# Differential attention two heads at a time, its scores in three banks

## The chip, the core and the metric

The kernel runs on one core of a Trainium2 chip. Its engines have queues of their own and meet at semaphores: TensorE (PE in the profile, its weight loads PEld), VectorE (DVE), ScalarE (ACT), GpSimd (POOL) and SyncE (SP), which issues the loads. The metric is the device time of one launch in microseconds.

## The reference

Two layers of two kinds of attention side by side, and after them a block with a convolution, pooling, cross attention and a feed-forward part, for 256 tokens of width 2048. The change touches the differential attention of the two layers alone: eight heads, each with two maps of 64 wide queries and keys, whose softmaxes are subtracted.

```python
def one_block(start):
    qb = lax.dynamic_slice_in_dim(q, start, BLOCK_Q, axis=1)
    s = jnp.einsum('bqhmd,bkhmd->bmhqk', qb, k).astype(jnp.float32) * scale
    ...
    s = jnp.where((dist >= 0)[None, None, None], s + bias[None, None], NEG_INF)
    p = jax.nn.softmax(s, axis=-1)
    w = p[:, 0] - lam * p[:, 1]
    return jnp.einsum('bhqk,bkhd->bqhd', w.astype(v.dtype), v)
```

The second attention (`_mla_attention`, called MLA below) takes its queries and keys from two latents of rank 512, `c_q` and `c_kv`, each times a weight matrix.

## The kernel before, in words

All weights stream through TensorE in units of 128 x 1024. SyncE loads a unit, ScalarE rounds it (`w_hi`, L406), VectorE subtracts (`w_lo`, L411), and TensorE multiplies in three passes (L448 to L450, L491 to L493). Four slots are reused in turn, and ScalarE and VectorE work three units ahead of TensorE. Products gather in `acc`, four banks in two pairs. A chunk of products takes the pair its number gives (even or odd), and may start only when an engine has evacuated the chunk two before it and counted it in `acc_free0` or `acc_free1` (`banks_free`).

A layer has 56 units for queries, keys, values and gate, then a loop of 32 steps, then 32 steps for the gate of MLA (z 0 to 31 here), then 32 for the output. The attention runs in the cracks of this stream. In the loop of 32 steps (u below, one unit each) TensorE multiplies: u 0 to 15 the latents, u 16 and 17 the rope key, u 18 to 21 the queries of MLA (one chunk each: 9, 10, 11, 12), u 22 and 23 the rope part of the queries, u 24 to 27 its keys (chunks 14 to 17), u 28 and 29, and u 30 and 31, its values (chunks 18, 19). ScalarE evacuates the query and key chunks with `copy_cols`, one step after the product. So u 20 (chunk 11) waits for the copy of u 18's chunk 9, and u 28 (chunk 18) for the copy of u 26's chunk 16.

Behind each unit stands what attention needs, written out by hand for each engine in the same loop. In the kernel before, head h takes four steps, u = 4h to 4h + 3:

- u = 4h: TensorE turns the last head's three weight blocks (L1152) and this head's two key blocks (L541); ScalarE copies both to SBUF.
- u = 4h + 1: TensorE multiplies the last head's weights with its values (L1158 to L1160) and makes this head's scores, two maps of 64 rows each in two banks (L1175). VectorE scales them, adds the bias and takes the maxima (`diff_max`, L2127 to L2135).
- u = 4h + 2: ScalarE takes the exponentials (L1694), where it stands in its queue behind the rounding of that step.
- u = 4h + 3: VectorE mixes the two maps (`diff_weights`, L2141 to L2147).

Everything that TensorE does between two units is called a burst below. Of the four banks of `aux`, `tb` (bank 0) holds turned blocks, `sc1` and `sc0` (banks 1, 2) the scores and `pv` (bank 3) turned weights and outputs. The latents are turned at u 10, 11, 19 and 21 (`C_TURN`), the rope key is summed on VectorE at u 17, just ahead of `diff_max`, and turned in `pv` at u 21.

The evacuation that the prediction speaks of, and its place in ScalarE's loop:

```python
for u in range(32):
    if u - 1 in QUERY_COLS:
        copy_cols(u - 1, C_QUERY + QUERY_COLS[u - 1], query_pair(QUERY_COLS[u - 1]))
    if u - 1 in KEY_COLS:
        copy_cols(u - 1, C_KEY + KEY_COLS[u - 1], key_pair(KEY_COLS[u - 1]))
    ...
    rounded(U_QKV + u)
    ...
    if r == 2:
        exps(h, ...)
```

Of the kernel before, what the change touches and what calls it, by code (L numbers as in the profile page):

```python
# [26 lines left out]
AX_X = mybir.AxisListType.X  # L27
# [76 lines left out]
TB_LAYER = 30  # L104
# [3 lines left out]
DIFF_TB = [2, 3, 4, 7, 8, 10, 12, 13]  # L108
C_TURN = {10: (0, 0, 5), 11: (0, 1, 6), 19: (1, 0, 9), 21: (1, 1, 11)}
QR_TB = 14  # L110
KEY_HEAD = 4
GATE_TURN = {12: (0, 0, 16), 13: (0, 1, 17), 20: (1, 0, 18), 21: (1, 1, 19), 28: (2, 0, 20), 29: (2, 1, 21),
             36: (3, 0, 22), 37: (3, 1, 23)}
X_TB = 24
MLA_PAIRS = HEADS // 2
# [3 lines left out]
HEAD_LAYER, PV_LAYER = HEADS + MLA_PAIRS, 2 * HEADS + 2 * MLA_PAIRS  # L119
# [132 lines left out]
def build(nc, dram, out):  # L252
# [12 lines left out]
    with ctx:  # L265
# [23 lines left out]
        kT = turn_f32[:, 1, 0:SEQ]  # L289
# [51 lines left out]
        roped, pool_step = sem("roped"), sem("pool_step")  # L341
        scores_ready, row_max, exps_done = sem("scores_ready"), sem("row_max"), sem("exps_done")
# [294 lines left out]
        s = b1("s", [P, 3 * SEQ])  # L637
        pT = b1("pT", [P, 2, 3 * P])
        lam_l = b1("lam_l", [P, 1])
        neg_max = b1("neg_max", [P, 4])  # L640
        row_sum = b1("row_sum", [P, 4])
        inv_sum = b1("inv_sum", [P, 4])
        mix_f = b1("mix_f", [P, 2])
# [221 lines left out]
        with nc.Block() as block:  # L865
# [136 lines left out]
            def _(pool):  # L1002
# [25 lines left out]
                for layer in range(LAYERS):  # L1028
# [5 lines left out]
                    pool.wait_ge(pv_free, layer * PV_LAYER + (2 * KEY_HEAD + 2))  # L1034
                    pool.wait_ge(tb_filled, layer * TB_LAYER + (TB_PRO + DIFF_TB[5] + 1))
# [27 lines left out]
                pool.wait_ge(row_max, (LAYERS - 1) * HEAD_LAYER + HEADS)  # L1063
# [19 lines left out]
            def _(pe):  # L1083
# [55 lines left out]
                for layer in range(LAYERS):  # L1139
# [7 lines left out]
                    def turn_weights(n, cols):  # L1147

                        if n > 0:
                            pe.wait_ge(pv_free, pv0 + n)  # L1150
                        for i, col in enumerate(cols):
                            mm = pe.transpose(pv[:, i * P:(i + 1) * P], s[:, col:col + P], ident[:, :])  # L1152
                        mm.then_inc(pv_filled, 1)
# [8 lines left out]
                    def outputs(n, val):  # L1162

                        pe.wait_ge(pv_free, pv0 + n)
                        weighted(0, 0, val).then_inc(pv_filled, 1)

                    def diff_scores(h):

                        pe.wait_ge(tb_free, tb0 + (DIFF_TB[h] + 1))
                        if h > 0:  # L1170
                            pe.wait_ge(row_max, head0 + h)
                        for col, q, keys in ((0, 1, SEQ), (SEQ, 0, P)):
                            for m, bank in ((0, sc1), (1, sc0)):
                                e = slice(m * DQ, (m + 1) * DQ)
                                mm = pe.matmul(bank[:, col:col + keys], diff_query(h)[e, q * P:(q + 1) * P],  # L1175
                                               kT[e, 0:keys], start=True, stop=True)
                        mm.then_inc(scores_ready, 1)

                    def diff_turn_weights(h):
                        pe.wait_ge(probs_ready, layer * HEADS + (h + 1))  # L1180
                        turn_weights(2 * h, (0, P, 2 * SEQ))

                    def diff_outputs(h):
                        outputs(2 * h + 1, lambda k: kz[:, k, WIDTH + h * DV:WIDTH + (h + 1) * DV])

                    def mla_scores(p):

                        if p == 0:
                            evacuated(pe, pairs, C_KEY + 2)
                            evacuated(pe, pairs, C_KEY + 3)  # L1190
                            pe.wait_ge(tb_free, tb0 + QR_TB + 2)
                            pe.wait_ge(pv_free, pv0 + 2 * HEADS)
                        pe.wait_ge(row_max, head0 + (HEADS + p))
# [20 lines left out]
                    def mla_turn_weights(p):  # L1214

                        pe.wait_ge(rsum_ready, layer * MLA_PAIRS + (p + 1))
                        pe.wait_ge(pv_free, pv0 + (2 * HEADS + 2 * p))
                        for i, bank in ((0, sc0), (1, pv)):
                            for n, col in enumerate((i * SEQ, i * SEQ + P, 2 * SEQ + i * P)):
                                mm = pe.transpose(bank[:, n * P:(n + 1) * P], s[:, col:col + P], ident[:, :])  # L1220
                        mm.then_inc(pv_filled, 1)

                    def mla_outputs(p):
# [4 lines left out]
                        pe.wait_ge(pv_free, pv0 + (2 * HEADS + 2 * p + 1))  # L1228
                        for i in range(2):
                            mm = weighted(i, i * SEQ, lambda k: value_of(2 * p + i, k))  # L1230
                        mm.then_inc(pv_filled, 1)

                    def diff_block(h):
                        return lambda i: kz[:, i, h * DV:(h + 1) * DV]
# [105 lines left out]
                    for u in range(32):  # L1340
# [22 lines left out]
                        h, r = u // 4, u % 4  # L1363
# [5 lines left out]
                        if r == 0:  # L1369
                            if h > 0:  # L1370
                                diff_turn_weights(h - 1)
                            turn(pe, tb0 + DIFF_TB[h], diff_block(h), blocks=2)
                        if r == 1:
                            if h == KEY_HEAD + 1:
                                pe.wait_ge(pv_free, pv0 + (2 * KEY_HEAD + 1))
                                evacuated(pe, pairs, 8)
                                for t in range(T):
                                    pe.matmul(pv[:, 3 * P + t * ROPE:3 * P + (t + 1) * ROPE],
                                              key_sum[:, t * P:(t + 1) * P], key_fold, start=True, stop=True)
                            if h > 0:  # L1380
                                diff_outputs(h - 1)
                            diff_scores(h)
                        if u in C_TURN:
                            j, t, use = C_TURN[u]
                            evacuated(pe, pairs, 6 + j)
# [4 lines left out]
                    for u in range(32):  # L1390
# [4 lines left out]
                        if u == 0:  # L1395
                            diff_turn_weights(HEADS - 1)
                            pe.wait_ge(roped, layer + 1)
                            turn(pe, tb0 + QR_TB, lambda i: qr[:, i % 2, (i // 2) * P:(i // 2 + 1) * P])
                        if u == 1:

                            pe.wait_ge(pv_free, pv0 + (2 * HEADS - 1))
                            for t in range(T):
                                pe.transpose(pv[:, (2 + t) * P:(3 + t) * P], kr2[:, t, :], ident[:, :])
                            diff_outputs(HEADS - 1)
# [3 lines left out]
                    for u in range(32):  # L1408
# [3 lines left out]
                        if u in (0, 6):  # L1412
                            pe.wait_ge(tb_free, tb0 + (22 if u == 0 else 23))
                        product_rows(pe, base, U_QKV + 64 + u, mT, 2 * i, 2, 512, c % 2, i == 0, i == 7,
                                     (lambda: pe.wait_ge(tb_free, tb0 + 24)) if u == 6 else None)
# [213 lines left out]
            def _(act):  # L1629
# [39 lines left out]
                for layer in range(LAYERS):  # L1669
# [28 lines left out]
                    def copy_weights(n):  # L1698

                        act.wait_ge(pv_filled, pv0 + (n + 1))  # L1700
                        if n < 2 * HEADS:
                            act.activation(pT[:, 0, :], pv[:, 0:3 * P], ACT.Copy).then_inc(pv_free, 1)
                        else:
                            act.activation(pT[:, :, :], aux[:, 2:4, 0:3 * P], ACT.Copy).then_inc(pv_free, 1)

                    def diff_output(h):


                        act.wait_ge(pv_filled, pv0 + (2 * h + 2))
                        for t, col, r in ((1, 0, 0), (0, P, 2)):  # L1710
                            o_step(act.activation(junk[:, 0:P], pv[:, col:col + P], ACT.Square,
                                                  scale=inv_sum[:, r:r + 1],
                                                  accum_out=sumsq_o[:, T * h + t:T * h + t + 1]))
                        for t, col, r in ((1, 0, 0), (0, P, 2)):
                            ins = act.activation(diff_output_of(h, t), pv[:, col:col + P], ACT.Copy,
                                                 scale=inv_sum[:, r:r + 1])
                        if h == KEY_HEAD:
                            for t in range(T):
                                ins = act.activation(kr[:, t, :], pv[:, 3 * P + t * ROPE:3 * P + (t + 1) * ROPE], ACT.Copy,
                                                     scale=rstd[:, t:t + 1])  # L1720
                        if h == HEADS - 1:
                            ins = act.activation(krT[:, :], pv[:, 2 * P:4 * P], ACT.Copy)
                        ins.then_inc(pv_free, 1)

                    def mla_output(p):

                        act.wait_ge(pv_filled, pv0 + (2 * HEADS + 2 * p + 2))
# [6 lines left out]
                    def z_heads(u):  # L1734

                        if u in MLA_TURN:
                            copy_weights(2 * HEADS + 2 * MLA_TURN[u])
                        if u in MLA_OUT:
                            mla_output(MLA_OUT[u])
                        if u - 1 in MLA_SCORE:  # L1740
                            exps(HEADS + MLA_SCORE[u - 1],
# [66 lines left out]
                    for u in range(32):  # L1808
# [17 lines left out]
                        h, r = u // 4, u % 4  # L1826
                        if r == 0:
                            if h > 0:
                                copy_weights(2 * (h - 1))
                            copy_bank(DIFF_TB[h], kT, tb[:, 0:SEQ])  # L1830
                        if r == 1 and h > 0:
                            diff_output(h - 1)
# [893 lines left out]
```

## Time and profile before

| | |
|---|---|
| median of 3 runs | 1917.46 us (1917.41 to 1917.61) |
| the profiled execution | 1917.76 us, its span 1915.6 us |
| granted TensorE clock over the span | 0.999 |
| TensorE matmul busy | 1906.9 us, 100% |
| VectorE, ScalarE, GpSimd busy | 75%, 56%, 3% |
| DMA | mean 189 GB/s |

Spans are read from starts: a matmul's own duration holds the way through the array, so what it costs the stream is the distance from its start to the next start. A row `x8` is a merged row: the passes that follow one another without a break.

### The profile page before, as it was taken

Reading aid. Unit: us, or ns where it says so; the run is one execution under the profiler, and the core shown is the slowest. Engines: PE = TensorE matmul, PEld = TensorE weight load, DVE = VectorE, ACT = ScalarE, POOL = GpSimd, SP = SyncE. Lnnn points to the kernel's source line nnn. Section 1 sums busy time; section 2 is a strip of 40 time slices with the busy share of each in tenths; the row PEclk is TensorE's granted clock in tenths of the full one; section 3 lists DMA queues with packets and bytes.
Section 4 is the critical chain, followed back from the end, with each engine's and each line's share of the span. In section 5 each row is a group of like instructions: output and inputs, shape, how many; then the busy total and the mean of one; then the engine's idle time right before and its main releaser. Section 6 shows DMA issues by size and latency. Waiting matters only on the chain.

```text
span 1915.6 us, 26983 instructions
## 1 busy us (share of the span) xinstructions
PE 1906.9 (100%) x9951; PEld 1627.5 (85%) x9951; DVE 1429.9 (75%) x1996; ACT 1071.7 (56%) x1586; POOL 48.7 (3%) x72
## 2 busy tenths in 40 slices
PE   9999999999999999999999999999999999999998
PEld 8888898888888898888888888888888888888886
DVE  6777675656777675655768766888878887889898
ACT  6655675655545676654644444555555555555554
POOL 1000030000000030000100000000000000000000
PEclk9999999999999999999999999999999999999999
DMA  9864545565665456545666455666666666665654
GB/s 342 303 217 133 148 151 161 166 207 178 216 205 164 145 156 192 152 159 185 211 191 186 152 176 177 189 183 187 196 188 190 191 186 187 190 223 192 204 194 172
DMA packets 260363, 361.38 MB, mean 189 GB/s; under 512 B 15504, under 2 KB 159072, under 8 KB 259760
## 3 DMA queue, kind: packets, MB, share of 16 engines
q1 hardware_dynamic: 258400, 353.15, 58.6%
q0 software_dynamic: 1584, 6.67, 1.0%
q8 instruction: 59, 0.97, 0.2%
q10 hardware_dynamic: 288, 0.33, 0.1%
q14 instruction: 32, 0.26, 0.0%
HBM read 356.95 MB, written 3.16 MB: 188 GB/s over the span
## 4 chain that ended last, share of the span: by engine, by line
PE 99%; DMA 0%; ACT 0%; DVE 0%; SPq 0%; issue 0%; DVEq 0%; ACTq 0%
PE acc L471 22%; PE acc L464 12%; PE acc L448 10%; PE acc L449 10%; PE acc L450 10%; PE acc L1281 3%; PE acc L1552 3%; PE acc L1554 3%; PE acc L1553 3%; PE acc L1261 3%; PE acc L1260 3%; PE acc L1259 3%; PE acc L1284 2%; PE aux L541 1%; PE acc L491 1%; PE aux L1552 1%
## 5 line engine op out<-in xcount | busy, mean ns | idle before, releaser
L411 DVE TENSOR_TENSOR sb_w_lo<-sb_stage,sb_w_hi 128x1024 fp32r<-128x1024 f32 x476 | 582.2, 1226 | 267.2 <-ACT sb_w_hi L406 260.3
L406 ACT ACTIVATE sb_w_hi<-sb_stage 128x1024 fp32r<-128x1024 f32 x476 | 503.2, 1058 | 380.4 <-PE acc L464 122.7
L471 PE MATMUL acc<-sb_xT,sb_w_hi 128*128 128x512 f32 x1856 | 445.8, 392 | 0.0
L471 PEld LDWEIGHTS acc<-sb_xT,sb_w_hi 128*128 128x128 f32 x1856 | 341.1, 188 | 65.5
L464 PEld LDWEIGHTS acc<-sb_xT,sb_w_lo 128*128 128x128 f32 x1856 | 238.7, 191 | 9.3
L464 PE MATMUL acc<-sb_xT,sb_w_lo 128*128 128x256 f32 x1856 | 243.1, 284 | 0.0
L448 PE MATMUL acc<-sb_w_hi,sb_mT 128*128 128x512 f32 x480 | 191.1, 398 | 0.0
L449 PE MATMUL acc<-sb_w_lo,sb_mT 128*128 128x512 f32 x480 | 187.3, 390 | 0.0
L450 PE MATMUL acc<-sb_w_hi,sb_mT 128*128 128x512 f32 x480 | 187.2, 390 | 0.0
L448 PE MATMUL acc<-sb_w_hi,sb_xT 128*128 128x512 f32 x384 | 154.7, 403 | 0.0
L449 PE MATMUL acc<-sb_w_lo,sb_xT 128*128 128x512 f32 x384 | 150.1, 391 | 0.0
L450 PE MATMUL acc<-sb_w_hi,sb_xT 128*128 128x512 f32 x384 | 150.0, 391 | 0.0
L448 PEld LDWEIGHTS acc<-sb_w_hi,sb_mT 128*128 128x128 f32 x480 | 90.2, 188 | 19.9 <-issue 1.0
L450 PEld LDWEIGHTS acc<-sb_w_hi,sb_mT 128*128 128x128 f32 x480 | 90.2, 188 | 19.3
L449 PEld LDWEIGHTS acc<-sb_w_lo,sb_mT 128*128 128x128 f32 x480 | 90.3, 188 | 17.5
L450 PEld LDWEIGHTS acc<-sb_w_hi,sb_xT 128*128 128x128 f32 x384 | 72.1, 188 | 15.5
L448 PEld LDWEIGHTS acc<-sb_w_hi,sb_xT 128*128 128x128 f32 x384 | 72.2, 188 | 14.4
L449 PEld LDWEIGHTS acc<-sb_w_lo,sb_xT 128*128 128x128 f32 x384 | 72.3, 188 | 13.3
L778 ACT ACTIVATE sb_w_hi<-sb_pair_stage 128x1024 fp32r<-128x1024 f32 (+1 forms) x50 | 48.2, 982 | 62.1 <-DVE sb_pair_stage L791 53.3
L2502 DVE SCALAR_TENSOR_TENSOR sb_ffn_tmp<-sb_ffn_tmp,sb_taps 128x254 f32<-128x254 f32 (+1 forms) x176 | 77.3, 481 | 2.5
L846 ACT ACTIVATE sb_w_hi<-sb_stage 128x1024 fp32r<-128x1024 f32 x46 | 48.1, 1058 | 41.2 <-DMA sb_stage<-w_in 17.0
L853 DVE TENSOR_TENSOR sb_w_lo<-sb_stage,sb_w_hi 128x1024 fp32r<-128x1024 f32 x46 | 55.4, 1222 | 20.4 <-ACT sb_w_hi L846 19.9
(493 smaller groups left out, 3026.0 us busy)
## 6 DMA issues: line engine op xcount, KB each, us to landing
sb_stage<-w_in SPq DMA_DIRECT2D x232, 512.0 KB, 4.4
sb_stage<-w_up SPq DMA_DIRECT2D x176, 512.0 KB, 3.7
sb_stage<-w_out SPq DMA_DIRECT2D x96, 512.0 KB, 4.2
sb_stage<-w_down SPq DMA_DIRECT2D x54, 512.0 KB, 6.6
sb_pair_stage<-w_down SPq DMA_DIRECT2D x34, 512.0 KB, 5.4
sb_kvb<-w_in SPq DMA_DIRECT2D x16, 512.0 KB, 6.3
sb_stage<-w_ukv SPq DMA_DIRECT2D x16, 512.0 KB, 4.1
sb_stage<-w_kv SPq DMA_DIRECT2D x15, 512.0 KB, 6.7
```

The costliest lines, as they stand in the source:

```text
L406: act.activation(w_hi[:, j % RING, 0:size], stage[:, j % RING, 0:size], ACT.Copy).then_inc(hi_ready, 1)
L411: dve.tensor_tensor(w_lo[:, j % RING, 0:size], stage[:, j % RING, 0:size], w_hi[:, j % RING, 0:size].bitcast(F32), ALU.subtract).then_inc( ...
L448: pe.matmul(o, x_hi, hi[:, k, :], start=first and k == 0, stop=False)
L449: pe.matmul(o, x_hi, lo[:, k, :], start=False, stop=False)
L450: mm = pe.matmul(o, x_lo, hi[:, k, :], start=False, stop=last and k == nk - 1)
L464: mm = pe.matmul(acc[:, 2 * pair + c, 0:SEQ], lo[:, k, c * P:(c + 1) * P], xT[:, k0 + k, 0, :], start=False, stop=False)
L471: mm = pe.matmul(acc[:, 2 * pair + c, :], hi[:, k, c * P:(c + 1) * P], both, start=first and k == 0, stop=last and k == 3)
L1259: pe.matmul(o, a(0), hi, start=start, stop=False)
L1260: pe.matmul(o, a(0), lo, start=False, stop=False)
L1261: return pe.matmul(o, a(1), hi, start=False, stop=stop)
L1552: pe.matmul(o, a(0), hi, start=start, stop=False)
L2502: last = dve.scalar_tensor_tensor(out=y[:, k, d:SEQ], in0=sum3[:, k, 0:SEQ - d], scalar=taps[:, 2 - d, half, k:k + 1], in1=y[:, k, d:SEQ], ...
```

## The change

Two heads form a pair, and a pair takes eight steps, u = 8p to 8p + 7. At u = 8p TensorE turns six weight blocks of the last pair and four key blocks; at u = 8p + 1 it makes both outputs and both heads' scores. The two late score blocks of the second head lie in `tb`, so that three banks hold scores, and a new semaphore, `upper_scores`, keeps the two row halves from writing one bank at once. Turned weights now fill half of `sc0` and `pv`. VectorE's maxima and mixing, and ScalarE's eight exponentials, come at u = 8p + 1, 8p + 5 and 8p + 2. The latents are turned at u 13, 14, 20 and 21, now after a wait for the pair's maxima, and the rope key has a burst at u 20. The order of `copy_cols` stays. The diff, cut to its core:

```diff
+PAIRS_OF_HEADS = HEADS // 2
+DIFF_TB = [2, 3, 6, 9]
+DIFF_PV = [0, 2, 5, 7]
+DIFF_MAX = {1: 0, 9: 1, 25: 3}
+DIFF_MIX = {5: 0, 13: 1, 21: 2, 29: 3}
+C_TURN = {13: (0, 0, 4), 14: (0, 1, 5), 20: (1, 0, 7), 21: (1, 1, 8)}
...
+                        scores(sc1, 0, 0, 0, 1, SEQ)
+                        scores(tb, SEQ, 1, 1, 1, SEQ).then_inc(upper_scores, 1)
+                        for h in range(2):
+                            scores(sc1, SEQ + h * P, h, 0, 0, P)
+                            scores(sc0, SEQ + h * P, h, 1, 0, P)
+                        pe.wait_ge(upper_scores, layer * PAIRS_OF_HEADS + (p + 1))
+                        scores(tb, 0, 1, 0, 1, SEQ)
+                        scores(sc0, 0, 0, 1, 1, SEQ).then_inc(scores_ready, 1)
...
-                        h, r = u // 4, u % 4
+                        p, r = u // 8, u % 8
...
                         if r == 0:
-                            if h > 0:
-                                diff_turn_weights(h - 1)
-                            turn(pe, tb0 + DIFF_TB[h], diff_block(h), blocks=2)
+                            if p > 0:
+                                diff_turn_weights(p - 1)
+                            turn(pe, tb0 + DIFF_TB[p], diff_block(p))
...
+                            if p > 0:
+                                diff_outputs(p - 1)
+                            diff_scores(p)
+                        if u == KEY_AT:
+                            pe.wait_ge(pv_free, pv0 + KEY_PV)
...
                         if u in C_TURN:
                             j, t, use = C_TURN[u]
+                            pe.wait_ge(row_max, head0 + (p + 1))
...
                         if r == 2:
-                            exps(h, ((0, SEQ, 0), (SEQ, SEQ, 1), (2 * SEQ, P, 2), (2 * SEQ + P, P, 3)))
+                            exps(p, [(n * SEQ, SEQ, n) for n in range(4)] + [(4 * SEQ + n * P, P, 4 + n) for n in range(4)])
...
+                        for h, scores, q, first, keys in ((0, aux[:, 1:3, 0:SEQ], 1, 0, SEQ), (1, two(tb), 1, 2 * SEQ, SEQ),
+                                                          (0, aux[:, 1:3, SEQ:SEQ + P], 0, 4 * SEQ, P),
+                                                          (1, aux[:, 1:3, SEQ + P:2 * SEQ], 0, 5 * SEQ, P)):
...
+                        dve.tensor_reduce(neg_max[:, 0:4], four(s[:, 0:4 * SEQ]), AX_X, ALU.max)
+                        step(dve.tensor_reduce(neg_max[:, 4:8], four(s[:, 4 * SEQ:6 * SEQ]), AX_X, ALU.max))
```

Lines of the changed kernel are 4 to 20 higher than those of the kernel before. TensorE's queue from the rope key's first unit (u 16) to its next product (u 18), before: L501 is the unit, L1152 and L541 the turned blocks, L1158 to L1160 the outputs and L1175 the scores.

```order
L501 MATMUL acc<-sb_xT,sb_w_hi 128x512 x7
L1152 MATMUL aux<-sb_ident,sb_s 128x128 [waits pv_free,probs_ready]
L1152 MATMUL aux<-sb_ident,sb_s 128x128 x2
L541 MATMUL aux<-sb_ident,sb_kz 128x128 [waits tb_free]
L541 MATMUL aux<-sb_ident,sb_kz 128x128
...
L1158 MATMUL aux<-sb_kz,sb_pT 128x128 [waits pv_free]
L1159 MATMUL aux<-sb_kz,sb_pT 128x128
L1160 MATMUL aux<-sb_kz,sb_pT 128x128
L1175 MATMUL aux<-sb_turn_f,sb_qa 128x256 [waits row_max,tb_free]
L1175 MATMUL aux<-sb_turn_f,sb_qa 128x256
L1175 MATMUL aux<-sb_turn_f,sb_qa 128x128 x2
L491 MATMUL acc<-sb_mT,sb_w_hi 128x256 [waits lo_ready,turn_lo,acc_free1]
```

The same place in the changed kernel (L1158 and L546 turn, L1164 to L1166 are the outputs, L1185 the scores):

```order
L1158 MATMUL aux<-sb_ident,sb_s 128x128 [waits pv_free,probs_ready]
L1158 MATMUL aux<-sb_ident,sb_s 128x128 x5
L546 MATMUL aux<-sb_ident,sb_kz 128x128 [waits tb_free]
L546 MATMUL aux<-sb_ident,sb_kz 128x128 x3
...
L1166 MATMUL aux<-sb_kz,sb_pT 128x128
L1185 MATMUL aux<-sb_turn_f,sb_qa 128x256 [waits row_max,tb_free]
L1185 MATMUL aux<-sb_turn_f,sb_qa 128x256
L1185 MATMUL aux<-sb_turn_f,sb_qa 128x128 x4
L1185 MATMUL aux<-sb_turn_f,sb_qa 128x256 [waits upper_scores]
L1185 MATMUL aux<-sb_turn_f,sb_qa 128x256
L496 MATMUL acc<-sb_mT,sb_w_hi 128x256 [waits lo_ready,turn_lo,acc_free1]
```

Both bursts carry twice as many blocks, and half as many bursts stand in the queue. ScalarE's queue from step u 18 into u 19, before: L406 rounds, L1822 scales the latent, L1694 are the exponentials, and L1797 is `copy_cols` of the chunk made at u 18.

```order
L406 ACTIVATE sb_w_hi<-sb_stage 128x1024 [waits unit_used,staged1]
L1822 ACTIVATE sb_qb<-sb_qb,sb_rstd_c 128x512 [waits c_rstd]
L1822 ACTIVATE sb_qb<-sb_qb,sb_rstd_c 128x512
L1694 ACTIVATE sb_s,sb_row_sum<-sb_s,sb_neg_max 128x256 [waits row_max]
L1694 ACTIVATE sb_s,sb_row_sum<-sb_s,sb_neg_max 128x256
L1694 ACTIVATE sb_s,sb_row_sum<-sb_s,sb_neg_max 128x128 x2
L1797 ACTIVATE sb_qb<-acc 128x512 [waits unit_used]
```

The same stretch in the changed kernel (L1709 are the exponentials, L1814 is `copy_cols`), and behind it u 26 into u 27, where the chunk goes to `kvb`:

```order
L411 ACTIVATE sb_w_hi<-sb_stage 128x1024 [waits unit_used,staged1]
L1839 ACTIVATE sb_qb<-sb_qb,sb_rstd_c 128x512 [waits c_rstd]
L1839 ACTIVATE sb_qb<-sb_qb,sb_rstd_c 128x512
L1709 ACTIVATE sb_s,sb_row_sum<-sb_s,sb_neg_max 128x256 [waits row_max]
L1709 ACTIVATE sb_s,sb_row_sum<-sb_s,sb_neg_max 128x256 x3
L1709 ACTIVATE sb_s,sb_row_sum<-sb_s,sb_neg_max 128x128 x4
L1814 ACTIVATE sb_qb<-acc 128x512 [waits unit_used]
...
L1709 ACTIVATE sb_s,sb_row_sum<-sb_s,sb_neg_max 128x256 x3
L1709 ACTIVATE sb_s,sb_row_sum<-sb_s,sb_neg_max 128x128 x4
L1814 ACTIVATE sb_kvb<-acc 128x512 [waits unit_used]
```

The copy stands where it stood, and eight exponentials stand ahead of it in place of four.

## Rows read from the trace of the kernel before

**Rows 1.** The page: engines, chain that ended last, costliest groups.

```profile
PE 1906.9 (100%) x9951; PEld 1627.5 (85%) x9951; DVE 1429.9 (75%) x1996; ACT 1071.7 (56%) x1586; POOL 48.7 (3%) x72
...
PE 99%; DMA 0%; ACT 0%; DVE 0%; SPq 0%; issue 0%; DVEq 0%; ACTq 0%
...
L411 DVE TENSOR_TENSOR sb_w_lo<-sb_stage,sb_w_hi 128x1024 fp32r<-128x1024 f32 x476 | 582.2, 1226 | 267.2 <-ACT sb_w_hi L406 260.3
L406 ACT ACTIVATE sb_w_hi<-sb_stage 128x1024 fp32r<-128x1024 f32 x476 | 503.2, 1058 | 380.4 <-PE acc L464 122.7
```

**Rows 2.** Timeline of PE at u 1: start us, duration us, instruction.

```profile
185.50 0.39 PE L449 MATMUL acc<-sb_w_lo,sb_xT 128*128 128x512 f32 x1
185.73 0.39 PE L450 MATMUL acc<-sb_w_hi,sb_xT 128*128 128x512 f32 x1
186.05 0.92 PE L1175 MATMUL aux<-sb_turn_f,sb_qa 64*128 64x256 f32 x8
186.90 0.50 PE L448 MATMUL acc<-sb_w_hi,sb_xT 128*128 128x512 f32 x1
```

**Rows 3.** Timeline of PE at u 5, outputs and scores, then two products.

```profile
198.50 0.38 PE L1158 MATMUL aux<-sb_kz,sb_pT 128*128 128x128 f32 x2
...
200.12 0.51 PE L448 MATMUL acc<-sb_w_hi,sb_xT 128*128 128x512 f32 x1
200.46 0.40 PE L449 MATMUL acc<-sb_w_lo,sb_xT 128*128 128x512 f32 x1
```

**Rows 4.** Timeline of PE at u 4: five turned blocks, the next product.

```profile
195.22 0.49 PE L1152 MATMUL aux<-sb_ident,sb_s 128*128 128x128 f32 x3
...
195.68 0.48 PE L448 MATMUL acc<-sb_w_hi,sb_xT 128*128 128x512 f32 x1
```

**Rows 5.** Timeline of PE at u 10: four turned blocks, the next product.

```profile
216.25 0.60 PE L541 MATMUL aux<-sb_ident,sb_qb 128*128 128x128 f32 x4
216.60 0.48 PE L448 MATMUL acc<-sb_w_hi,sb_xT 128*128 128x512 f32 x1
```

**Rows 6.** Timeline of PE at u 24: five turned blocks, the next product.

```profile
262.64 0.55 PE L1152 MATMUL aux<-sb_ident,sb_s 128*128 128x128 f32 x3
...
263.30 0.39 PE L491 MATMUL acc<-sb_mT,sb_w_hi 128*128 128x256 f32 x1
```

**Rows 7.** Timeline of all engines, scores of u 17 to the end of u 19.

```profile
239.03 0.39 PE L491 MATMUL acc<-sb_mT,sb_w_hi 128*128 128x256 f32 x1
...
240.19 0.74 DVE L2127 SCALAR_TENSOR_TENSOR sb_s<-aux,sb_par,sb_bias 128x512 f32<-128x512 f32 x1
...
242.41 0.17 DVE L2135 TENSOR_SCALAR sb_neg_max<-sb_neg_max 128x4 f32<-128x4 f32 x1
...
242.61 0.51 ACT L1694 ACTIVATE sb_s<-sb_s,sb_neg_max 128x256 f32<-128x256 f32 x1 [0.16 <-DVE sb_neg_max L2135]
...
244.39 0.57 ACT L1797 ACTIVATE sb_qb<-acc 128x512 f32<-128x512 f32 x1
...
244.89 0.60 PE L541 MATMUL aux<-sb_ident,sb_qb 128*128 128x128 f32 x4
```

**Rows 8.** Timeline of all engines, scores of u 25 to the start of u 28.

```profile
267.89 0.39 PE L491 MATMUL acc<-sb_mT,sb_w_hi 128*128 128x256 f32 x1
...
268.01 0.75 DVE L2127 SCALAR_TENSOR_TENSOR sb_s<-aux,sb_par,sb_bias 128x512 f32<-128x512 f32 x1 [0.37 <-PE aux L1175]
...
269.93 1.29 POOL L1050 TENSOR_TENSOR sb_kz<-sb_qb,sb_rope 128x512 f32<-128x512 f32 x1
...
270.23 1.01 DVE L2135 TENSOR_SCALAR sb_neg_max<-sb_neg_max 128x4 f32<-128x4 f32 x1
...
271.28 0.51 ACT L1694 ACTIVATE sb_s<-sb_s,sb_neg_max 128x256 f32<-128x256 f32 x1 [1.10 <-DVE sb_neg_max L2135]
...
273.06 0.57 ACT L1797 ACTIVATE sb_kvb<-acc 128x512 f32<-128x512 f32 x1
...
273.74 0.44 PE L448 MATMUL acc<-sb_w_hi,sb_mT 128*128 128x512 f32 x1
```

More of the change, by code:

```diff
@@ L1179, in diff_turn_weights, with diff_scores, scores @@
[L1179 to L1184, printed above, removed]
+                        for i in range(2):
+                            mm = weighted(i, i * SEQ, lambda k: val(i, k))
+                        mm.then_inc(pv_filled, 1)
+                    def diff_scores(p):
+                        pe.wait_ge(tb_free, tb0 + (DIFF_TB[p] + 1))
+                        if p > 0:
+                            pe.wait_ge(row_max, head0 + p)
+                        def scores(bank, col, h, m, q, keys):
+                            e = slice(m * DQ, (m + 1) * DQ)
+                            return pe.matmul(bank[:, col:col + keys], diff_query(2 * p + h)[e, q * P:(q + 1) * P],
+                                             kT[e, h, 0:keys], start=True, stop=True)
+                        scores(sc1, 0, 0, 0, 1, SEQ)
[6 more added lines that the diff above has]
+                        scores(sc0, 0, 0, 1, 1, SEQ).then_inc(scores_ready, 1)
@@ L1214, in mla_turn_weights @@
                     def mla_turn_weights(p):
[L1216 to L1221, printed above, removed]
+                        pe.wait_ge(rsum_ready, layer * PAIRS_OF_HEADS + (p + 1))
+                        turn_weights(MLA_PV + 2 * p, lambda i: (i * SEQ, i * SEQ + P, 2 * SEQ + i * P))
                     def mla_outputs(p):
@@ L1227, in mla_outputs, with diff_block @@
                             evacuated(pe, pairs, C_VALUE + 1)
[L1228 to L1234, printed above, removed]
+                        outputs(MLA_PV + 2 * p + 1, lambda i, k: value_of(2 * p + i, k))
+                    def diff_block(p):
+                        return lambda i: kz[:, i % 2, (2 * p + i // 2) * DV:(2 * p + i // 2 + 1) * DV]
                     def gated_block(g, t):
@@ L1711, in diff_output @@
+                    def diff_output(p):
+                        act.wait_ge(pv_filled, pv0 + (DIFF_PV[p] + 2))
+                        tiles = [(i, t, i * SEQ + (1 - t) * P, 2 * i + 4 * (1 - t)) for i in range(2) for t in (1, 0)]
+                        for i, t, col, r in tiles:
+                            n = T * (2 * p + i) + t
                             o_step(act.activation(junk[:, 0:P], pv[:, col:col + P], ACT.Square,
-                                                  scale=inv_sum[:, r:r + 1],
@@ L1716, in diff_output @@
                                                  scale=inv_sum[:, r:r + 1])
[L1717 to L1722, printed above, removed]
+                        if p == PAIRS_OF_HEADS - 1:
+                            ins = act.activation(krT[:, :], sc1[:, 0:SEQ], ACT.Copy)
@@ L1723, in diff_output, with key_rows @@
+                        ins.then_inc(pv_free, 1)
+                    def key_rows():
+                        act.wait_ge(pv_filled, pv0 + (KEY_PV + 1))
+                        for t in range(T):
+                            ins = act.activation(kr[:, t, :], pv[:, t * ROPE:(t + 1) * ROPE], ACT.Copy,
+                                                 scale=rstd[:, t:t + 1])
                         ins.then_inc(pv_free, 1)
                     def mla_output(p):
[L1727 removed]
+                        act.wait_ge(pv_filled, pv0 + (MLA_PV + 2 * p + 2))
```

178 lines of the change are left out of this document (81 added, 97 removed).

## The prediction

> **What bounds the kernel now.** I read the page first. TensorE is busy for 1906.9 us of a span of 1915.6, and it holds 99% of the chain that ended last [rows 1]; its granted clock is 0.999 over the span. So the stream of TensorE is the time. Whatever shortens it is gained whole, and whatever makes it stand still is lost whole, however idle the other engines are on average. Two questions follow: what a burst costs the stream, and whether another engine, now asked for two heads' work in one piece, still delivers before TensorE needs it. For the first I read TensorE's timeline at single bursts [rows 2 to 6]. For the second I looked for waits of TensorE that today end with almost nothing to spare, in the timeline of all engines [rows 7, 8].
>
> **What a burst costs.** Products in the stream start 0.23 us apart (185.50, 185.73), or 0.227 over many. The score burst of one head starts 0.32 after the last product, 0.09 more than that, and the next product comes 0.85 after its first start [rows 2], so it costs 0.94. With the last head's outputs ahead of it the burst takes 1.61 from start to start [rows 3], so the outputs add 0.67 for six passes of 0.11, and bring no fixed cost. Turned blocks: five in 0.46 [rows 4], four in 0.35 [rows 5], so 0.11 a block less 0.08 once. After a burst the first product holds the second back to 0.34 instead of 0.23 [rows 3], a tail of 0.11; I take 0.12 with what follows, and 0.11 to 0.17 as its bounds.
>
> A 128 column pass costs 0.107, so a 256 column one 0.21 by proportion. Each head's scores are four passes of each length in two lanes side by side, 2 x 0.21 + 2 x 0.107 = 0.64. The other 0.30 of the 0.94 is paid for each burst, for changing to the half-height form and back.
>
> **The gain.** Per layer:
> - Eight score bursts become four: 4 x 0.30 = 1.20 us.
> - Bursts of any kind in the stretch fall from 21 to 14: seven tails of 0.12, 0.84 us (0.77 to 1.19).
> - Three of those bursts were of turned blocks alone, each with its 0.08 hidden, which is lost: 0.24 us. The number of turned blocks, outputs and scores stays.
> - At u 24 five turned blocks take 0.66 instead of 0.46 [rows 4, 6], because head 5's weights are mixed only just before. Between a pair's scores and the turn of its weights lie seven steps, not three: 0.20 us gained.
> - Cost of `upper_scores`: the second half of a pair's scores waits for its first two blocks. Behind them four short pairs of passes are queued, 0.43 us, which cover most of the way through the array. From 0 to 0.10 a pair; I take 0.05, so 0.2 us.
>
> Together a gain of 1.20 + 0.84 - 0.24 + 0.20 - 0.20 = 1.80 us a layer.
>
> **Stall at u 20.** This is where I expect the gain to be lost. u 20 needs the bank pair that u 18 filled. ScalarE frees it with the copy L1797 at 244.39, which ends at 244.96, just as TensorE finishes u 19 (the next burst starts at 244.89) [rows 7]. Today the latent's four blocks, 0.35, stand between and hide this. In the changed kernel they move behind u 20, so TensorE wants the banks at what is 244.89 here. And the copy comes later: it stands in ScalarE's queue behind the exponentials, which wait for the maxima.
> - Maxima: 240.19 to 242.41, 2.22 us, for one head [rows 7]. Two heads double the columns, but the two reductions and the final multiply stay one instruction each. I take 1.88 more (1.7 to 2.22).
> - Exponentials: 242.61 to 244.39, 1.78 us for four [rows 7]. Eight: 1.78 more.
> - VectorE begins the maxima 1.16 after the scores (239.03 to 240.19), since its steps for the latent's norm and the rope key's sum stand ahead. The scores now end 0.67 + 0.64 = 1.31 later against the units, that other work about 0.4 later, as ScalarE copies larger blocks before it. So the maxima begin about 0.25 after the scores, 0.9 less (0.5 to 1.05).
>
> The copy ends at 244.96 + 1.88 + 1.78 - 0.9 = 247.72 on this scale, against 244.89: TensorE stands for 2.8 us (2.4 to 3.5).
>
> **Stall at u 28.** The same shape. u 28 needs the pair freed by the copy at 273.06, done at 273.63, and starts at 273.74 [rows 8], with 0.11 to spare. Add 1.88 + 1.78 and take off 0.11: 3.55. Here the maxima begin 0.12 after the scores (267.89 to 268.01), so nothing comes back on that side. The row shows one thing more: the final multiply took 1.01 us instead of 0.17, while GpSimd ran L1050 from 269.93 to 271.22 [rows 7, 8]. GpSimd's rope work starts with u 24 and now lies earlier against the scores, so the multiply may meet a shorter instruction or none; I take 0.25 off: 3.3 us (2.7 to 4.4).
>
> The Trainium skill's page "SBUF — State Buffer", section "Who interferes with whom", says that of a VectorE instruction in a two-port form and a GpSimd instruction the one that comes second is blocked until the first ends. By that rule the multiply loses nothing or the rest of one GpSimd instruction. The rows agree as far as they go: it ended when L1050 did.
>
> **Smaller waits.** The eight exponentials also stand before the rounding of the next unit. From the scores' end: maxima 4.1, exponentials 3.6, rounding 1.06, subtraction 1.23 [rows 1], so the unit five steps after a pair's first score step is ready about 10.2 us after the scores, and wanted after four units of twelve products each, 2.72 us, so 10.9. It holds, by 0.7. The second turn of the latent at u 14 waits for VectorE's reading of the first, behind its doubled mixing. The two come about together; between 0 and one subtraction, 1.2. I take 0.2 us.
>
> **The sum.** A layer: -1.80 + 2.8 + 3.3 + 0.2 = +4.5 us. The two layers run the same code: +9.0 us. The profiled execution took 1917.76 (its span 1915.6 and 2.2 around it), 0.3 over the median of the runs. So 1926.8 for an execution like the profiled one, and 1926.5 for the median.
>
> **The rivals.**
> 1. *The copies come in time, and the gain stays.* This needs both copies to end no later than the products before them. The bursts then give 2 x 1.80, so 1913.9. For it speaks the page, where ScalarE is busy for 56% only [rows 1]. Against it stand the two copies with no slack today, and 3.6 us of work added in one row in front of each. Chance 0.08.
> 2. *Stalls of half that size*, because VectorE starts the maxima at once, reductions are cheaper, or one of the two places is relieved: 1 to 1.5 us at each, then -1.80 + 2.5 + 0.2 = +0.9 a layer, 1919.3. The count of bursts and of copies would be right, their balance even. Chance 0.09.
> 3. *The weights run dry as well.* The margin of 0.7 us above is used up in the steps behind the exponentials (u 6, u 14, u 20), because ScalarE still has the outputs of the last pair (eight instructions instead of four) ahead of the rounding. One unit late by 0.5 to 1.5 at two places a layer: +2 to +6 more, 1930. Chance 0.13.
> 4. *The clock drops.* A TensorE that stands still for 3 us might be granted 1.2 GHz instead of 2.4 when it goes on. The trace has no such idle time inside its span to read this from, and its clock is full throughout. If one unit of 2.72 us ran at half speed behind each of the four stalls, 4 x 2.7 = 11 us more, 1937. The Trainium skill's page "TensorE: Matmul & The Clock Gate", section "Why this matters for your kernels", warns of exactly such gaps between bursts; no row here shows one. Chance 0.05.
>
> **How the numbers follow.** The forecast has the remaining 0.65, with a range of its own of 1923 to 1930.5: stalls of 5.1 to 7.9 us a layer in place of 6.1, and a gain between 1.7 and 2.2. The range for 8 in 10 takes in most of rivals 2 and 3: 1919.5 to 1931.5. About 0.2% (3.8 us) is what a measurement of this kernel can tell from no change. Faster by more than that is rival 1, whose 1913.9 lies at the bound, 0.05. Within it are the rest of rival 1, and rival 2, 0.12. Slower has 0.83.
>
> **What would show it.** In the profile after, TensorE's idle time, nearly zero today, should be some 12 us, in four gaps of about 3 us, ahead of the first product of u 20 and of u 28 in each layer, with the copy (L1814) on `acc` named as what ended them, and in the chain of waits ScalarE and VectorE should appear with L1709 and L2149. Score bursts with outputs should take about 2.9 us from start to start (1.61 + 0.67 + 0.64), turned blocks 1.0 for ten. At u 24 no lateness should be left. I am wrong if TensorE's idle time stays below 2 us a layer, or if gaps of this size stand elsewhere, at `lo_ready` or at `upper_scores`.

## The result, and the profile after

| | median us | lowest to highest | runs | against before, 95% interval |
|---|---|---|---|---|
| before | 1917.43 | 1917.19 to 1918.31 | 6 | |
| after | 1928.35 | 1927.65 to 1930.26 | 6 | 1.0058 [1.0046, 1.0069] |

The changed kernel is slower by 10.9 us. The forecast was 9.1 us and the same sign. The profiled execution took 1928.3 us with a span of 1925.6, 10.0 us more than the span of before.

The page of the kernel after, its engines, the chain that ended last, and the one group of products with idle time ahead of it:

```profile
PE 1905.4 (99%) x9951; PEld 1626.0 (84%) x9951; DVE 1419.5 (74%) x1956; ACT 1069.5 (56%) x1570; POOL 44.2 (2%) x72
...
PE 96%; DVE 2%; ACT 1%; issue 0%; DMA 0%; SPq 0%; DVEq 0%; ACTq 0%
...
L453 PE MATMUL acc<-sb_w_hi,sb_mT 128*128 128x512 f32 x480 | 191.3, 399 | 5.1 <-ACT sb_kvb L1814 5.1
```

TensorE is busy for 1.5 us less than before [rows 1], in a span that is 10.0 longer. So it now stands still for 20.2 us instead of 8.7 (the span less the busy time), 11.5 us more. The waits of TensorE in the kernel after, line waited for, total us, times, longest, say where:

```profile
PE acc L453 <- ACT sb_kvb L1814: 5.1, 2, 2.5
PE acc L496 <- ACT sb_qb L1814: 5.1, 2, 2.5
PE acc L1092 <- POOL sb_turn_f L1008: 1.0, 1, 1.0
PE acc L1102 <- ACT sb_mT L1652: 0.6, 1, 0.6
PE acc L1121 <- ACT sb_w_hi L411: 0.4, 1, 0.4
PE aux L546 <- DVE sb_turn_f L557: 0.4, 2, 0.2
```

Four waits, twice before u 20 (L496) and twice before u 28 (L453), each ended by the copy L1814. All engines around u 20 of the first layer, kernel after, as [rows 7] of before (start us, duration us):

```profile
239.17 2.19 DVE L2149 SCALAR_TENSOR_TENSOR sb_s<-aux,sb_par,sb_bias 128x512 f32<-128x512 f32 x4
...
243.24 0.17 DVE L2156 TENSOR_SCALAR sb_neg_max<-sb_neg_max 128x8 f32<-128x8 f32 x1
...
243.44 0.51 ACT L1709 ACTIVATE sb_s<-sb_s,sb_neg_max 128x256 f32<-128x256 f32 x1 [0.52 <-DVE sb_neg_max L2156]
...
244.78 0.28 PE L498 MATMUL acc<-sb_mT,sb_w_lo 128*128 128x256 f32 x1
...
246.97 0.57 ACT L1814 ACTIVATE sb_qb<-acc 128x512 f32<-128x512 f32 x1
...
247.59 0.39 PE L496 MATMUL acc<-sb_mT,sb_w_hi 128*128 128x256 f32 x1 [2.53 <-ACT sb_qb L1814]
```

The last product of u 19 starts at 244.78. The next would start at 244.90, 0.12 later, and starts at 247.59: a stall of 2.69 us, from start to start. (The 2.5 of the list of waits runs from a modelled end.) The maxima take 4.07 us up to the start of their last step where they took 2.22, the exponentials 3.53 where they took 1.78, and the copy stands behind both. The same around u 28, as [rows 8]:

```profile
270.08 2.19 DVE L2149 SCALAR_TENSOR_TENSOR sb_s<-aux,sb_par,sb_bias 128x512 f32<-128x512 f32 x4 [1.97 <-PE aux L1185]
...
271.75 0.74 POOL L1061 TENSOR_TENSOR sb_kz<-sb_kz 128x256 f32<-128x256 f32 x1
...
274.15 0.17 DVE L2156 TENSOR_SCALAR sb_neg_max<-sb_neg_max 128x8 f32<-128x8 f32 x1
...
274.36 0.51 ACT L1709 ACTIVATE sb_s<-sb_s,sb_neg_max 128x256 f32<-128x256 f32 x1 [1.26 <-DVE sb_neg_max L2156]
...
275.69 0.28 PE L498 MATMUL acc<-sb_mT,sb_w_lo 128*128 128x256 f32 x1
...
277.88 0.57 ACT L1814 ACTIVATE sb_kvb<-acc 128x512 f32<-128x512 f32 x1
...
278.51 0.50 PE L453 MATMUL acc<-sb_w_hi,sb_mT 128*128 128x512 f32 x1 [2.54 <-ACT sb_kvb L1814]
```

From 275.69 to 278.51 are 2.82, so this stall is 2.70 us. The final multiply takes 0.17 us here, not 1.01: GpSimd had ended at 272.49.

The first scores of MLA start at 303.56 (before 300.12) in layer 0, and at 747.85 (before 737.82) in layer 1. So layer 0 costs 3.44 us up to there, and layer 1 another 6.59. The difference of 3.2 stands behind the two stalls of layer 1. TensorE's timeline there, kernel after:

```profile
718.47 0.28 PE L498 MATMUL acc<-sb_mT,sb_w_lo 128*128 128x256 f32 x1
721.28 0.79 PE L453 MATMUL acc<-sb_w_hi,sb_mT 128*128 128x512 f32 x1 [2.54 <-ACT sb_kvb L1814]
721.88 0.63 PE L454 MATMUL acc<-sb_w_lo,sb_mT 128*128 128x512 f32 x1
722.30 0.63 PE L455 MATMUL acc<-sb_w_hi,sb_mT 128*128 128x512 f32 x1
...
724.44 0.44 PE L454 MATMUL acc<-sb_w_lo,sb_mT 128*128 128x512 f32 x1
724.71 0.39 PE L455 MATMUL acc<-sb_w_hi,sb_mT 128*128 128x512 f32 x1
```

Products start 0.43 apart instead of 0.23 for 3.2 us, then the normal pace returns. Four stretches of the same kernel, the first two behind the stalls of layer 0, the others inside the slow parts of layer 1. The columns are the stretch, its length, the busy time of PE, PEld, DVE, ACT and POOL, the granted clock (1.00 is 2.4 GHz, 0.50 is 1.2 GHz), DMA share and GB/s:

```profile
247.60:250.60 3.00, 3.00 (x25) 3.00 (x26) 1.23 (x1) 2.32 (x3) 0.00 (x0) 1.00 0.45 147
278.50:281.50 3.00, 2.99 (x13) 2.50 (x14) 1.86 (x2) 2.33 (x3) 0.00 (x0) 1.00 0.02 8
690.40:692.90 2.50, 2.50 (x14) 2.50 (x13) 0.61 (x1) 0.78 (x1) 0.00 (x0) 0.50 0.42 129
721.90:724.40 2.50, 2.50 (x7) 1.96 (x6) 1.98 (x2) 1.71 (x3) 0.00 (x0) 0.50 0.53 197
```

So of four stalls two were followed by a stretch at 1.2 GHz, some 3.3 us long. Half of such a stretch is lost: 1.6 to 1.7 us each, 3.3 us in this execution.

The bursts of the kernel after, u 8 with ten turned blocks and u 9 with outputs and scores:

```profile
206.80 0.82 PE L1158 MATMUL aux<-sb_ident,sb_s 128*128 128x128 f32 x6
207.46 0.60 PE L546 MATMUL aux<-sb_ident,sb_kz 128*128 128x128 f32 x4
207.81 0.47 PE L453 MATMUL acc<-sb_w_hi,sb_xT 128*128 128x512 f32 x1
...
210.65 0.38 PE L1164 MATMUL aux<-sb_kz,sb_pT 128*128 128x128 f32 x2
...
212.07 1.58 PE L1185 MATMUL aux<-sb_turn_f,sb_qa 64*128 64x256 f32 x16
213.59 0.50 PE L453 MATMUL acc<-sb_w_hi,sb_xT 128*128 128x512 f32 x1
```

1.01 and 2.94 us from start to start.

### The profile page after: what moved, and what is told of

Same layout as the page of the kernel before. It is cut to its first block, busy times and chain, and to the rows that moved or that the text cites. A ratio compares the mean times of both kernels' runs of the same rounds, so it can differ in the third digit from the quotient of the medians.

```text
span 1925.6 us, 26917 instructions
## 1 busy us (share of the span) xinstructions
PE 1905.4 (99%) x9951; PEld 1626.0 (84%) x9951; DVE 1419.5 (74%) x1956; ACT 1069.5 (56%) x1570; POOL 44.2 (2%) x72
## 4 chain that ended last, share of the span: by engine, by line
PE 96%; DVE 2%; ACT 1%; issue 0%; DMA 0%; SPq 0%; DVEq 0%; ACTq 0%
PE acc L476 22%; PE acc L469 12%; PE acc L453 10%; PE acc L455 10%; PE acc L454 10%; PE acc L1295 3%; PE acc L1568 3%; PE acc L1567 3%; PE acc L1569 3%; PE acc L1275 3%; PE acc L1273 3%; PE acc L1274 3%; PE acc L1298 2%; PE aux L546 1%; ACT sb_s L1709 1%; PE aux L1567 1%
## 5 line engine op out<-in xcount | busy, mean ns | idle before, releaser
L453 PE MATMUL acc<-sb_w_hi,sb_mT 128*128 128x512 f32 x480 | 191.3, 399 | 5.1 <-ACT sb_kvb L1814 5.1
L453 PE MATMUL acc<-sb_w_hi,sb_xT 128*128 128x512 f32 x384 | 153.6, 400 | 0.0
L453 PEld LDWEIGHTS acc<-sb_w_hi,sb_mT 128*128 128x128 f32 x480 | 90.6, 189 | 25.3 <-ACT sb_kvb L1814 5.5
L453 PEld LDWEIGHTS acc<-sb_w_hi,sb_xT 128*128 128x128 f32 x384 | 72.2, 188 | 14.9 <-issue 1.3
```

Source lines behind the costliest of these rows:

```text
L453: pe.matmul(o, x_hi, hi[:, k, :], start=first and k == 0, stop=False)
```

## The experiments

**The copy ahead of the exponentials.** Nothing else is moved; the exponentials stay ahead of the same rounding.

```diff
                         if u - 1 in KEY_COLS:
                             copy_cols(u - 1, C_KEY + KEY_COLS[u - 1], key_pair(KEY_COLS[u - 1]))
+                        if u in (19, 27):
+                            exps(u // 8, ...)
...
-                        if r == 2:
+                        if r == 2 and u + 1 not in (19, 27):
                             exps(p, ...)
```

> The changed kernel with one edit: on ScalarE the exponentials of pairs 2 and 3 stand behind the copy of u 18's and u 26's banks (still ahead of the next rounding), nothing else moves. Theory A, the copy's place behind eight exponentials is the whole stall: the banks are free by about 243.4 where TensorE wants them at 244.9, and by 274.0 against 275.8, so both waits of 2.7 us go in both layers, and with them the two stretches at 1.2 GHz that the profile shows behind the stalls of layer 1 (1.3 and 1.6 us). 1928.35 - 4 x 2.7 - 2.9 = 1914.6 us, faster than before, which is what the bursts alone give (1917.4 - 2 x 1.93 = 1913.6). Theory B, the wait only changes its name: the exponentials still stand ahead of the rounding, and TensorE, coming 2.7 us earlier, meets weights that are not ready (at lo_ready, u 22 and u 30), so 1 to 2 us a place come back: 1918 to 1922 us. Theory C, the maxima set it: no change, 1928.

Measured: 1913.55 us (11 runs, 1912.94 to 1914.09), 0.9978 [0.9969, 0.9987] of before, so faster than either kernel. In its list of waits only the start of the program and u 14 are left:

```profile
PE acc L1092 <- POOL sb_turn_f L1008: 1.0, 1, 1.0
PE aux L546 <- DVE sb_turn_f L557: 0.4, 2, 0.2
```

ScalarE in this kernel: the copy now stands in time that ScalarE spent waiting for the maxima, and the exponentials begin 0.03 after it.

```profile
242.32 0.61 ACT L1814 ACTIVATE sb_qb<-acc 128x512 f32<-128x512 f32 x1
242.96 0.51 ACT L1709 ACTIVATE sb_s<-sb_s,sb_neg_max 128x256 f32<-128x256 f32 x1
...
246.49 1.05 ACT L411 ACTIVATE sb_w_hi<-sb_stage 128x1024 fp32r<-128x1024 f32 x1
```

The wait did not change its name (theory B). The maxima held the copy back only through its place behind the exponentials, not by themselves (theory C): here they are no shorter, and the wait is gone. The whole price was the order of two pieces of work in one queue.

**One place at a time.** The same edit with `(19,)` and with `(27,)` alone.

> The changed kernel with the copy ahead of the exponentials at u 20's place alone (pair 2). Theory A: only the stalls of 2.7 us before u 20 go, two of them, and the slow stretch behind the one of layer 1 (1.3 us): 1928.35 - 5.4 - 1.3 = 1921.7 us; the waits before u 28 stay at 2.7 us each. Theory B (wait changes its name): 1924 to 1926 us. If half the four-place effect is carried by the clock rather than by the waits, less than 4 us are gained.

> The changed kernel with the copy ahead of the exponentials at u 28's place alone (pair 3). Theory A: the two stalls of 2.7 us before u 28 go, and the slow stretch of 1.6 us behind the one of layer 1: 1928.35 - 5.4 - 1.6 = 1921.4 us; the waits before u 20 stay. Theory B: 1923 to 1926 us. Together with the run that mends u 20 alone it says whether the two places add up to the run that mends both.

Measured: the copy first ahead of u 20 alone 1921.99 us (1.0021 [1.0012, 1.003]), ahead of u 28 alone 1921.16 us (1.0018 [1.0009, 1.0027]), each 11 runs. Over 1913.55 that is 8.4 and 7.6 us for two remaining stalls of 2.70, 5.4 us. The rest is 3.0 and 2.2 us, and in the profiled executions the clock fell behind both stalls in the one (after 272.45 and 712.62) and behind one of two in the other (after 683.01). The places add up: 8.4 + 7.6 = 16.0 against 14.8 for both, 1.2 apart, less than one stretch at 1.2 GHz. (The profiled execution of the second kernel took 1920.11 us, near the lowest of its runs.)

**Doses.** Three kernels that make the four stalls shorter or longer. First, four exponentials ahead of the copy and four behind it; then six and two; then all eight and the next rounding ahead of it.

```diff
-                        if r == 2:
+                        if r == 2 and p < 2:
                             exps(p, ...)
+                        if u in (18, 26):
+                            first_exps(p)
...
                             copy_cols(u - 1, C_KEY + KEY_COLS[u - 1], key_pair(KEY_COLS[u - 1]))
+                        if u in (19, 27):
+                            last_exps(u // 8)
```

`first_exps` holds the four long exponentials (six: and two short ones), `last_exps` the others. The third kernel:

```diff
                     for u in range(32):
+                        if u in (19, 27):
+                            rounded(U_QKV + u)
                         if u - 1 in QUERY_COLS:
...
-                        rounded(U_QKV + u)
+                        if u not in (19, 27):
+                            rounded(U_QKV + u)
```

> The changed kernel with the exponentials of pairs 2 and 3 split: the four long ones ahead of the copy, the four short ones behind it. A dose of about half. Theory A: the copies end at 243.44 + 1.99 + 0.57 = 246.0 and 274.36 + 1.99 + 0.57 = 276.9 where TensorE wants 244.9 and 275.8, so stalls of 1.1 us are left at each of four places, 1.6 us less than 2.7: 1928.35 - 6.4 = 1922.0 us if the clock behind the stalls stays as it is, 1919.1 us if stalls of this length bring no slow stretch. Theory C (the wait is not made by the exponentials): no change from 1928.

> The changed kernel with the exponentials split six to two around the copy: four long and two short ones ahead of it, two short ones behind. A dose between the half one (1918.46 us, stalls of 1.15 us) and the whole. The stalls are 1.15 + 0.77 = 1.9 us at four places: 1913.55 + 4 x 1.9 = 1921.2 us if the clock stays at 2.4 GHz behind them, as it did behind stalls of 1.15 us; with 1.5 us more for each place where it falls, so 1922.7 to 1927.2 us if it falls at one to four.

> The changed kernel with the copy of u 18's and u 26's banks one place later still in ScalarE's queue: behind the exponentials and behind the rounding of the next unit (1.04 us in the profile). A larger dose. The copies end 1.0 us later, so the stalls at four places grow from 2.7 to 3.7 us: 1928.35 + 4.0 = 1932.4 us if TensorE's clock falls behind as many stalls as before (theory A, time is the sum of the stalls), and up to 1934.4 us if it now falls behind all four (theory D, a part of the loss is the clock, about 1.5 us each time, and longer stalls bring it more often). If stalls were filled from a buffer elsewhere: less than 1930 us.

Measured, with the stall as the traces have it (the gap between starts less 0.12), and the places behind which the profiled execution shows 1.2 GHz (the times are medians, the places are those of one execution each):

| ahead of the copy | stall, us | time, us | over 1913.55 | 4 stalls | rest | places at 1.2 GHz |
|---|---|---|---|---|---|---|
| nothing | 0 | 1913.55 | 0 | 0 | 0 | 0 |
| 4 exponentials | 1.16 | 1918.46 | 4.9 | 4.6 | 0.3 | 0 of 4 |
| 6 | 1.93 | 1923.62 | 10.1 | 7.7 | 2.4 | 1 of 4 |
| 8 (kernel after) | 2.70 | 1928.35 | 14.8 | 10.8 | 4.0 | 2 of 4 |
| 8 and a rounding | 3.64 | 1935.89 | 22.3 | 14.6 | 7.7 | 4 of 4 |

Against before: 1.0004 [0.9995, 1.0013], 1.0031 [1.0019, 1.0043], 1.0095 [1.0079, 1.011] for the three. The stalls came out as computed. The time is more than their sum, and the rest grows with the places at 1.2 GHz, as theory D had it. But 1935.89 lies above the 1934.4 that theory D gave as its most: its 1.5 us a place was too small for the largest dose. There the granted clock was 0.50 behind all four:

```profile
248.80:253.80 5.00, 5.00 (x25) 5.00 (x25) 0.38 (x1) 1.03 (x2) 0.00 (x0) 0.50 0.44 145
283.40:288.20 4.80, 4.80 (x13) 3.67 (x12) 3.16 (x8) 0.84 (x1) 0.00 (x0) 0.50 0.59 160
698.00:701.20 3.20, 3.20 (x17) 3.20 (x16) 0.00 (x0) 0.18 (x1) 0.00 (x0) 0.50 0.55 181
730.80:735.50 4.70, 4.70 (x13) 3.64 (x12) 3.08 (x8) 0.76 (x1) 0.00 (x0) 0.50 0.69 194
```

In three of these four places the clock fell while TensorE still stood (over 247.0 to 248.0, with its next product at 248.46, the grant is 0.69 on average), and 5.7, 5.5 and 5.3 us of products ran slow; behind the third stall it was 3.4 us. Half of that, 10.0 us, is an estimate of what this execution lost to the clock. It took 1937.91 us, the slowest of four, so the row of the table, with its median, has less.

Each profiled execution can be weighed by itself. Its span, less the 1911.1 of the kernel with the copies first and less its stalls, leaves 1.1, 2.3, 3.7 and 9.8 us for the four doses. Half of the slow stretches is 0, 1.7, 3.3 and 10.0 us. Some 0.5 us more come from the start of the program, which took that much longer in these executions (the last passes of L1121 start at 14.83 to 14.92, against 14.40). What is then left over is 0.6 us or less in each.

**The bursts' price by itself.** In the kernel with the copies first, the first pair of long score passes goes back to a burst of its own, ahead of the last three products of its unit (ahead of the last two of u 17, the rope key, and of the last six short ones of u 25).

```diff
+                if early and (k, t) == (nk - 1, T - 1):
+                    early.pop()()
...
+                        if u % 8 == 1:
+                            early.append(lambda: diff_scores(u // 8, True))
...
-                        scores(sc1, 0, 0, 0, 1, SEQ)
-                        scores(tb, SEQ, 1, 1, 1, SEQ).then_inc(upper_scores, 1)
+                        if first:
+                            scores(sc1, 0, 0, 0, 1, SEQ)
+                            scores(tb, SEQ, 1, 1, 1, SEQ).then_inc(upper_scores, 1)
+                            return
```

> The kernel with both copies ahead of the exponentials (1913.55 us), and in it the scores of a pair in two bursts again, as the kernel before had them: the first pair of long score passes goes ahead of the last three products of the same unit, the others stay at its end with the outputs. Same passes, eight score bursts a layer become... in all eight more bursts in the program. Theory A, a half-height burst costs 0.30 us for the change of form and 0.12 us of tail: 8 x 0.42 = 3.4 us more, 1917.0 us, which takes back most of what the changed kernel gains on TensorE. Theory B, a burst costs its tail alone, and the gain was in something else: 8 x 0.12 = 1.0 us, 1914.5 us.

Measured: 1917.52 us (11 runs), 1.0001 [0.9992, 1.001] of before. That is 3.97 us over 1913.55, 0.50 for each of eight bursts: theory A's mechanism, and more than its 3.4 us. In the trace at u 9 of this kernel:

```profile
210.44 0.70 PE L1193 MATMUL aux<-sb_turn_f,sb_qa 64*128 64x256 f32 x4
211.07 0.50 PE L457 MATMUL acc<-sb_w_hi,sb_xT 128*128 128x512 f32 x1
211.41 0.39 PE L458 MATMUL acc<-sb_w_lo,sb_xT 128*128 128x512 f32 x1
...
211.87 0.38 PE L1172 MATMUL aux<-sb_kz,sb_pT 128*128 128x128 f32 x2
...
214.38 0.50 PE L457 MATMUL acc<-sb_w_hi,sb_xT 128*128 128x512 f32 x1
```

The early burst delays the stream by 0.72 (the product at 211.07 would have come at 210.35), the late one takes 2.51 from start to start. Together 3.23 against 2.94 for the merged one: 0.29 for the change of form. The second tail adds 0.11 (0.34 from 211.07 to 211.41 instead of 0.23). The burst of u 20 takes 1.02 in this kernel and 0.78 in the one with the copies first, 0.06 a pair; no run shows why. These make 0.46 of the 0.50.

**The same reordering in the kernel before.** A control.

```diff
+                        if u in (19, 27):
+                            exps(u // 4, ...)
...
-                        if r == 2:
+                        if r == 2 and u + 1 not in (19, 27):
                             exps(h, ...)
```

> The kernel before, with the same reordering that mends the changed one: the exponentials of the heads of u 18 and u 26 stand behind the copy of these units' banks on ScalarE. A control. Theory A: before has no wait of TensorE there (0 and 0.1 us to spare), so there is nothing to gain, 1917.5 us, and the 4.1 us by which the changed kernel with the copies first (1913.55 us) beats it come from the bursts alone. Rival E: the reordering is a gain of its own in either kernel, so 1914 to 1916 us here, and the merging of the bursts gives little.

Measured: 1917.52 us (11 runs) against 1917.52, 0.9999 [0.999, 1.0008]. The reordering gives nothing where there is no stall. So the 4.1 us by which the kernel with the copies first beats before are not the reordering's. Nearly all of it, 3.97 us, goes when the score bursts are parted again.

**The wait at u 14.** Added to the kernel with the copies first:

```diff
-C_TURN = {13: (0, 0, 4), 14: (0, 1, 5), 20: (1, 0, 7), 21: (1, 1, 8)}
+C_TURN = {12: (0, 0, 4), 14: (0, 1, 5), 20: (1, 0, 7), 21: (1, 1, 8)}
```

> The kernel with both copies ahead of the exponentials (1913.55 us), and in it the first turn of the latent in u 12 instead of u 13, so that VectorE reads it before it mixes pair 1's weights; the second stays in u 14. Theory A: TensorE's wait of 0.34 us ahead of the turned blocks of u 14, seen in the profile in both layers, goes: 1912.9 us. Rival: VectorE's reading at u 12 only pushes the mixing and the next subtraction back, and the 0.34 us come back at u 13 or u 16: no change, 1913.5 us.

Measured: 1912.86 us (10 runs, 1912.31 to 1913.55), 0.9976 [0.9966, 0.9985] of before. In its trace the turned blocks of u 14 start 0.23 behind the product, where the kernel after has 0.57 (227.55 to 228.12):

```profile
227.27 0.39 PE L455 MATMUL acc<-sb_w_hi,sb_xT 128*128 128x512 f32 x1
227.50 0.60 PE L546 MATMUL aux<-sb_ident,sb_qb 128*128 128x128 f32 x4
```

The wait is gone, and the kernel's list of waits has none in the loop in its place, only 0.6 us at the start of the program. That the 0.69 us of the medians are this wait (2 x 0.34) rests on that trace; the ranges of the two kernels' runs overlap. It is the fastest kernel of the study, 4.8 us (0.24%) under before.

## Why the prediction held, point by point

- **The bound, and the places.** Right. The gaps stand before u 20 and u 28 of both layers, the copy named as their end, and moving that copy alone takes them away.
- **Stall at u 20.** 2.8 forecast, 2.69 measured. The terms held: maxima 1.85 longer (1.88), exponentials 1.75 (1.78), begun 0.12 behind the scores (0.25).
- **Stall at u 28.** 3.3 forecast, 2.70 measured. The mis-sized term is what GpSimd gives back: I took 0.25 of the multiply's 0.84 off, all of it went, since GpSimd's work ended 1.7 us before (272.49 against 274.15). The rule of the Trainium skill's page "SBUF — State Buffer", section "Who interferes with whom", allowed this as one of its two cases, a multiply that loses nothing; the rows agree, 0.17 us with GpSimd idle.
- **The gain.** 1.80 a layer forecast. With both copies first the kernel gains 4.1 us in all with the wait at u 14 in it, and 4.8 without, so 2.4 a layer. The change of form costs what was forecast, 0.29 against 0.30, but merging two score bursts gives 0.50, not 0.42. `upper_scores` costs less than put: from the first score of u 1 to the next product are 1.51 us (186.12 to 187.63), where one head's 0.85 [rows 2] and 0.64 make 1.49, so 0.02 a pair and not 0.05. At u 24 no lateness is left: ten turned blocks take 1.01 from start to start (263.05 to 264.06), as at u 8. Outputs and scores together take 2.94, forecast as 2.9.
- **Smaller waits.** u 14 stands 0.34 us, forecast 0.2. No wait at `lo_ready` in the loop (rival 3), so the margin of the weights held. It was put too small: the four terms of the text, 4.1, 3.6, 1.06 and 1.23, add up to 10.0, not to 10.2, and leave 0.9 us, not 0.7.
- **The clock (rival 4).** Here the text was wrong in its odds. It was given 0.05 as a case of its own, at 2.7 us for each of four stalls. It came at two of them in the profiled execution, at some 1.6 us each, 3.3 us. In the medians 4.0 us are left beside the stalls (14.8 less 10.8); that is a remainder, and the longer start of the program is in it too. So the forecast is near in part by luck: -3.2 (the gain with the wait at u 14 in it) + 12.2 (stalls) = 9.0 was forecast, and -4.1 + 10.8 + 4.0 = 10.7 is how the runs divide the 10.9. The gain was 0.9 us larger and the stalls 1.4 us smaller than put, and the clock, which the sum had at nothing, made up for both. With the clock at full pace throughout it would have been -4.1 + 10.8, 1924.1, the low part of the forecast's own range. The Trainium skill's page "TensorE: Matmul & The Clock Gate", section "HAM oscillation — how this bites in real kernels", says that a TensorE left idle between groups of products comes back at the lower clock. The traces agree at some of the places, 0.50 granted behind stalls of 1.93 to 3.64 us; but the page speaks of longer gaps than most of these, and there the rows decide.
- **Rivals 1 and 2.** Neither came true, but their prices were about right. Rival 1 said what the kernel would be if the copies came in time, 1913.9. The kernel with the copies first measured 1913.55. Rival 2 said 1919.3 for stalls of half the size; with 1.16 us each the kernel measured 1918.46.

## What to carry to other kernels

Before two units of work are merged, list what stands behind them in each engine's queue, and for each such item who waits for it and with how much to spare. A copy that frees a bank belongs ahead of work that only becomes longer, when its input is ready first: here one exchange turned +0.58% into -0.22%. And where the engine that bounds the kernel was made to stand still, the price was the stall plus, at some of the places, a stretch at the lower clock.

## What the runs showed of the hardware

- TensorE's granted clock fell to 0.50 behind single stalls of 1.93 to 3.64 us in a stream that was otherwise full: behind none of four of 1.16 us, one of four of 1.93, two of four of 2.70 in the kernel after (three of four in the two kernels with the copy first at one place), four of four of 3.64. From 3.2 to 5.7 us of products ran slow each time, over 5 us only behind stalls of 3.64. Which of equal stalls is hit varied: both of layer 1 in one kernel, one in each layer in another. What picks them stays open.
- The fall need not come at the stall's end. Three of the four stalls of 3.64 us had it before they ended. In the kernel after, the stall before u 20 of layer 1 ended at 688.86, twelve products ran at the full pace, and the slow ones begin at 690.38; the one before u 28 was followed by slow products at once.
- A half-height burst of four passes delays a stream of full-height products by 0.72 us (u 9 of the kernel with the scores apart). Splitting one burst into two costs 0.29 us for the change of form; with the longer tail and the rest it is 0.50 us for each of eight further bursts.
